# Low-rank projection of the decay gates: three token blocks at once on three groups of 32 columns

## What is computed

```
h   = RMSNorm_pre(x) * (1 + scale) + shift
z   = h @ W_in         # columns: q | k | v | g | lr_f | lr_b | u
la_f = log_sigmoid(lr_f @ w_a2[0] + b_a2[0]) / 16      # per token, 256 channels
la_b = log_sigmoid(lr_b @ w_a2[1] + b_a2[1]) / 16
o_f, s_f = gla(q, k, v, la_f, s0_fwd)                  # chunked scan
o_b, s_b = gla(flip(q), flip(k), flip(v), flip(la_b), s0_bwd)
y = concat(rmsnorm(o_f + flip(o_b)) * silu(g), fourier(u)) @ W_out
```

## Time and profile before

| | us |
|---|---|
| three runs | 1488.44, 1487.04, 1477.68 |
| median | 1487.04 |
| span of the profiled execution, first to last instruction | 1476.2 |
| PE busy in it | 1252.9 |
| DVE busy in it | 747.0 |
| ACT busy in it | 425.2 |
| POOL busy in it | 256.6 |

### The profile page before, as it was taken

One profiled execution on the slowest core, in us unless ns is written; L12 is line 12 of the kernel. 1 busy time (PEld: TensorE's weight loads), 2 busy tenths in 40 slices (PEclk: granted clock), 3 DMA queues, 4 the chain that ended last, 5 costly groups with the idle time before them and its releaser, 6 DMA issues.

```text
span 1476.2 us, 18755 instructions
## 1 busy us (share of the span) xinstructions
PE 1252.9 (85%) x7319; PEld 736.4 (50%) x7319; DVE 747.0 (51%) x1093; ACT 425.2 (29%) x736; POOL 256.6 (17%) x416
## 2 busy tenths in 40 slices
PE   3449999999862338976879999999999999999995
PEld 2225568886651314433445454454554545546442
DVE  3364583892652434755545444444545354454537
ACT  4354352322111215643333032130311312213103
POOL 1111120430212111112211111202112111121104
PEclk9779999999785768988989999999999999999998
DMA  9822011434300220000011110101011010111003
GB/s 294 266 92 63 29 58 37 147 112 147 118 29 0 105 109 29 1 14 16 29 57 34 54 57 30 58 30 57 32 55 58 29 57 29 58 39 48 29 0 128
DMA packets 70751, 97.24 MB, mean 66 GB/s; under 512 B 3077, under 2 KB 53386, under 8 KB 70666
## 3 DMA queue, kind: packets, MB, share of 16 engines
q1 hardware_dynamic: 70666, 96.04, 19.9%
HBM read 86.33 MB, written 9.70 MB: 65 GB/s over the span
## 4 chain that ended last, share of the span: by engine, by line
PE 47%; issue 2%; DVE 1%; POOL 1%; ACT 1%; POOLq 0%; ACTq 0%; DVEq 0%
PE bank L1202 47%; ACT bank L866 1%; POOL region L833 1%; DVE region L2055 0%; POOL small L757 0%; DVE region L2026 0%; POOL small L677 0%; DVE region L1953 0%; DVE ghb L1953 0%; ACT whi L554 0%; DVE region L2057 0%; DVE region L1942 0%; POOL small L755 0%; ACT region L1115 0%; ACT region L1120 0%
## 5 line engine op out<-in xcount | busy, mean ns | idle before, releaser
L1202 PE MATMUL bank<-region,whi 128*128 128x384 f16 (+1 forms) x1872 | 460.4, 328 | 47.8 <-issue 31.9
L1202 PE MATMUL bank<-whi,region 128*128 128x512 f16 (+1 forms) x1872 | 487.9, 348 | 8.9 <-DVE region L1909 8.9
L1202 PE MATMUL bank<-wlo,region 128*128 128x512 f16 (+1 forms) x936 | 325.3, 348 | 0.0
L1202 PE MATMUL bank<-region,wlo 128*128 128x384 f16 (+1 forms) x936 | 307.2, 328 | 0.0
L1202 PEld LDWEIGHTS bank<-region,whi 128*128 128x128 f16 (+1 forms) x1872 | 183.3, 98 | 174.5 <-issue 37.8
L1202 PEld LDWEIGHTS bank<-whi,region 128*128 128x128 f16 x1872 | 184.2, 98 | 170.5 <-DVE region L1909 9.8
L1202 PE MATMUL bank<-region 128*128 128x512 f16 (+8 forms) x802 | 176.0, 386 | 64.0 <-DVE region L1858 34.3
L2026 DVE SCALAR_TENSOR_TENSOR region<-bank,small,region 128x512 f32<-128x512 f32 x144 | 106.7, 749 | 180.5 <-PE bank L1202 180.1
L554 ACT ACTIVATE whi<-stage,small 128x2048 f16<-128x2048 f32 (+1 forms) x42 | 82.3, 1960 | 338.3 <-PE bank L1202 291.1
L1202 PEld LDWEIGHTS bank<-region 128*128 128x128 f16 (+4 forms) x802 | 112.7, 171 | 119.5 <-issue 48.2
L702 POOL PARTITION_ALL_REDUCE small<-small x45 | 76.3, 1695 | 407.1 <-DVE small L537 335.1
(11 more groups left out here) (152 smaller groups left out, 900.7 us busy)
## 6 DMA issues: line engine op xcount, KB each, us to landing
stage<-in_w_fc SPq DMA_DIRECT2D x32, 1024.0 KB, 5.2
stage<-in_w_ada SPq DMA_DIRECT2D x16, 1024.0 KB, 5.3
region<-in_w_ada SPq DMA_DIRECT2D x8, 1024.0 KB, 12.0
stage<-in_w_in SPq DMA_DIRECT2D x8, 1024.0 KB, 5.4
x_with_position<-region SPq DMA_DIRECT2D x9, 512.0 KB, 4.9
region<-x_with_position SPq DMA_DIRECT2D x9, 512.0 KB, 9.1
out_dram<-region SPq DMA_DIRECT2D x9, 512.0 KB, 2.6
region<-in_x_sample SPq DMA_DIRECT2D x8, 512.0 KB, 10.6
```

Of the source, the lines that this page charges most:

```text
L1202: return nc.tensor.matmul(out, lhsT, rhs, start=start, stop=stop, skip_group_check=True)
```

## The change

The three tiles of the rank stage become one bank of 96 rows: block t goes to rows 32t to 32t+31, by products placed on the columns 32t to 32t+31 of the array. The loop order is depth, term, block, so the three blocks' products of one slice and one term stand next to each other. The stage waits once for `s_tl` at 5 and halfway at 6. ACT evicts the bank in one instruction to `lrS`, now 96 rows by 384 columns. `wa2` is kept three times, at rows 0, 32 and 64, so that the logits of block t read the partitions from 32t on. Its blocks come by six small loads instead of two, POOL clears 96 rows instead of 32, and the semaphore that counts the loads is waited for at 112 instead of 48. Ring A loses two places in its list.

```diff
@@ -153,7 +153,7 @@
 
     def z_uses(i):
         if i == LR:
-            return [("z", i, 0, t) for t in range(TB)]
+            return [("z", i, 0, 0)]
         if i in TFORM:
             return [("z", i, m, t) for t in range(TB) for m in range(2)]
         return [("z", i, 0, j) for j in range(NT)]
@@ -358,8 +358,9 @@
         acc = R1[:].rearrange("p (j n) -> p j n", j=NT)
 
 
-        wa2 = R34[0:2 * RANK, 4608:4608 + 512]
-        lrS = R34[0:2 * RANK, 5120:5120 + TOK]
+        LRP = 2 * RANK * TB
+        wa2 = R34[0:LRP, 4608:4608 + 512]
+        lrS = R34[0:LRP, 5120:5120 + TBW]
 
 
         s_2h = sem("h2_high")
@@ -604,8 +605,10 @@
             sp.dma_start(ghb[:], a["g_head"][0].rearrange("h v -> (h v)").partition_broadcast(P)).then_inc(s_misc, 16)
 
             sp.wait_ge(s_wa2, 1)
-            for d in range(2):
-                sp.dma_start(wa2[RANK * d:RANK * d + RANK, 256 * d:256 * d + 256], a["w_a2"][0, d]).then_inc(s_misc, 16)
+            for t in range(TB):
+                for d in range(2):
+                    r = 2 * RANK * t + RANK * d
+                    sp.dma_start(wa2[r:r + RANK, 256 * d:256 * d + 256], a["w_a2"][0, d]).then_inc(s_misc, 16)
 
             for j in range(NT):
                 x_ready(sp, j)
@@ -777,7 +780,7 @@
             h_scale(0)
             for i in range(1, len(zin)):
                 chunk_scale(i)
-            pool.wait_ge(s_misc, 48)
+            pool.wait_ge(s_misc, 16 * (1 + 2 * TB))
             for r in range(2 * NT + 1):
                 if r < 2 * NT:
                     pool.wait_ge(s_ge, r + 1)
@@ -958,9 +961,8 @@
                 if i == LR:
                     for key in z_uses(i):
                         bank = take_z(key)
-                        t = key[3]
-                        nc.scalar.activation(lrS[:, TBW * t:TBW * t + TBW], bank[0:2 * RANK, 0:TBW], ACT.Copy,
-                                             scale=wcof[0:2 * RANK, i % 8:i % 8 + 1]).then_inc(A.read(key), 1)
+                        nc.scalar.activation(lrS, bank[0:LRP, 0:TBW], ACT.Copy,
+                                             scale=wcof[0:LRP, i % 8:i % 8 + 1]).then_inc(A.read(key), 1)
                 elif i == Q:
                     evac_t(i, qT)
                 elif i == K:
@@ -1288,15 +1290,30 @@
                              (lambda k: wh[:, k, :], lambda k: wl[:, k, :]))
 
             def logits(k):
-                pe.wait_ge(s_misc, 48)
-                for t in range(TB):
-                    A.wait_read(pe, ("z", LR, 0, t))
+                pe.wait_ge(s_misc, 16 * (1 + 2 * TB))
+                A.wait_read(pe, z_uses(LR)[0])
                 for d in range(2):
                     for t in range(TB):
                         key = ("la", d, k, t)
                         bank = B.open(pe, key)
-                        mm(bank[:, 0:TBW], wa2[:, 256 * d + P * k:256 * d + P * k + P], lrS[:, TBW * t:TBW * t + TBW],
+                        r = 2 * RANK * t
+                        mm(bank[:, 0:TBW], wa2[r:r + 2 * RANK, 256 * d + P * k:256 * d + P * k + P], lrS[r:r + 2 * RANK, :],
                            True, True).then_inc(B.filled(key), 1)
+
+            def rank_tile(key):
+
+                wh, wl = pair(LR)
+                bank = A.open(pe, key)
+                for k in range(KT):
+                    if k == KT // 2:
+                        pe.wait_ge(s_tl, 2 * TB)
+                    for n, (w, H) in enumerate(((wh, HTh), (wh, HTl), (wl, HTh))):
+                        for t in range(TB):
+                            r = 2 * RANK * t
+                            ins = nc.tensor.matmul(bank[r:r + 2 * RANK, 0:TBW], w[:, k, :], H[:, k, TBW * t:TBW * t + TBW],
+                                                   start=k == 0 and n == 0, stop=k == KT - 1 and n == 2,
+                                                   tile_position=(0, r), skip_group_check=True)
+                return ins
 
             for i in range(G_A):
                 pe.wait_ge(s_wlo, i + 1)
@@ -1304,9 +1321,8 @@
                     if i in TFORM:
                         _, _, m, t = key
                         if i == LR:
-
-                            pe.wait_ge(s_tl, 2 * t + 1)
-                            ins = up_tile(key, 0, i, m, t, HTh, HTl, 2 * RANK, lambda: pe.wait_ge(s_tl, 2 * t + 2))
+                            pe.wait_ge(s_tl, 2 * TB - 1)
+                            ins = rank_tile(key)
                         else:
                             ins = up_tile(key, 0, i, m, t, HTh, HTl)
                     else:
@@ -1771,7 +1787,7 @@
                 elif i == V_B:
                     fold()
             step(V.memset(Srf, 0.0))
-            dve.wait_ge(s_misc, 48)
+            dve.wait_ge(s_misc, 16 * (1 + 2 * TB))
             for what, n in gate_events:
                 if what == "z":
                     if n == 0:
```

## The result

| | before | after |
|---|---|---|
| median of 12 runs each, us | 1483.88 | 1474.08 |
| lowest and highest, us | 1477.02, 1488.44 | 1468.13, 1481.41 |
| ratio of after to before, with its 95% interval | | 0.9929 [0.9911, 0.9947] |
| profiled execution: span, its own time, us | 1476.2 | 1470.9, 1472.70 |

The change takes 0.71% off, 10.5 us by the ratio (the two medians are 9.8 apart); the interval runs from 0.53 to 0.89%. The forecast was 1484.7 us, 2.3 us less than the median of the three runs known then.

A forecast was written before the change was run, and what follows sets the result against it. TensorE (PE) was taken as the bound from Q's first product at 106.65 us, VectorE (DVE) releasing Q before. Q's clock (-1.3) and logits (-1.0) gave 1487.0 - 2.3 = 1484.7 us, range 1475.4 to 1492.2 us.

The forecast's parts named there:

- The rank stage: Before Q: a packed group of three costs one product, ending near 103.9 us; the 48 products saved gain nothing themselves.
- The second rival: Rank stage into Q's start: column groups run one after another, +3.8 us, 1490.8 us; chance 0.13.
- the third: Rank stage: weight loads stand between the products, Q 2.0 us late, 1488.0 us; chance 0.05.
- The step on the clock: Packed rank stage: low clock for 3.1 us of work (10 groups), then full; pause before Q 2.7 us at most.
- Q's first products: Start of Q: after the shorter pause its first 9 products run at the full clock, 1.3 us gained.
- The logits: Both sets of logits: three products run side by side until banks bind, 0.5 us gained a set, 1.0 us in all.
- it holds PE for 0.68 us: Logits: the sixth product, starting when a bank frees at 134.33 us, ends at 135.0 us instead of 135.53.
- The sum: Whole kernel: -1.3 - 1.0 = -2.3 us, put against the runs' median of 1487.0 us, giving 1484.7 us.
- The rest, at nothing: Single eviction, POOL's clearing of 96 rows, four more loads and ring places: 0 us, at worst 1.0 us from POOL.
- A microsecond taken from its queue there is a microsecond of the program: From Q's first product, for 260 us: PE is the bound, so its savings count fully if what follows only moves along.
- The forecast's case: Whole kernel: 2.3 us faster, 1484.7 us; chance 0.6.
- The first rival: Q and logits: nothing gained is on the path, Q starts at the low clock, logits wait for banks, 1487.0 us; chance 0.22.

## Why the prediction was wrong, and where it was right

**The rank stage: right, but for the clock.** Threes side by side, loads inside the products, no time gained by the 48 products saved themselves. The second rival (column groups one after another) and the third (loads between the products) are refuted by the pitch of 0.32 us. The rule of the Trainium skill behind the third ("TensorE: Matmul & The Clock Gate", "Part 3: Packing small matmuls") is contradicted by the loads of three column groups, 0.18 us together, that start while products of the same rows run. The step on the clock was wrong in its size for this trace: the low clock lasted to about 107 us, 5.75 us of work, not 3.1, so the stage ends at 108.2, and the pause is 1.56 us instead of 2.7. In the two further traces of after it is 2.75 and 2.03 us, near the forecast's, and Q's first products are at the full clock there too:

```profile
107.77 0.50 PE L1204 MATMUL bank<-region,whi 128*128 128x384 f16 x2 [2.75 <-DVE wlo L563]
```

In all traces Q is at the low clock, from its start or soon behind it, after pauses of 3.9 to 4.6 us, and at the full clock throughout after pauses of up to 2.75 us.

**Q's first products: right in the trace, mis-sized as a term.** "All of it", 1.3 us, is what the two first traces show (24.82 to 23.50). But in four traces of before Q takes 24.82 to 26.38 us, 25.56 in the mean: the term is 2.1 us. In the other three Q loses 1.7 to 2.9 us, as the low clock lasts longer than the 2.80 us read off the first.

**The logits: right in the trace, wrong as a term.** 3.51 us and 3.58 us hold PE instead of twice 4.06, 1.0 us together, and the banks bind as worked out; counted from Q's first product, K starts 1.87 us earlier, where 1.8 was forecast. The step that failed is "it holds PE for 0.68 us": that is the price at the full clock. In three of four traces of before the clock falls in these products, and then they and the first microseconds of the next projection cost more. From the logits to the end of the projections the four traces of before take 197.48 us in the mean, the three of after 192.85: the term measured 4.6 us, not 1.0.

**The sum: the step that cost the forecast.** "A difference this small is put against the median" joined a gain read in one execution to a median that this execution doesn't stand for. Its span of 1476.2 us was 1.5 us under the fastest run then known, and the prediction said so, but took it for what lies around the span. Where a run's own time and span are both known, they lie 1.8 us apart (1472.70 and 1470.9). The execution's time was thus about 1478 us, nearly the fastest of twelve and 6 us under their median. The 10.8 us from its span to the median of the first three were taken as what lies around the span, and as scatter. It should have been read as: something costs this kernel some 6 to 9 us in its usual execution that this trace doesn't show. Not all of that is the cost that the change takes away. The span is 6.2 us under the mean of the other three traces of before: 3.0 of this lie ahead of h's first low half, where nothing is edited (it starts at 83.9 us instead of 86.9), and of the 6.5 us between Q and the end of the projections some 3 are lost again in the stretch behind.

**"The rest, at nothing": right on the edits.** POOL and then SP in order of time, after, answering to the earlier trace rows:

```profile
67.10 0.52 POOL L779 MEMSET region<- 96x512 f32 x1
...
67.65 2.65 SPq L611 DMA_DIRECT2D region<-in_w_a  x6
```

96 rows are cleared in the time of 32 (0.515 us before), and six loads take 2.65 us instead of 2.4 as worked out, with Q's pace still set by DVE. The one eviction takes 0.58 us instead of 1.48 and nobody waits for it.

**"A microsecond taken from its queue there is a microsecond of the program": not borne out.** The prediction made it hang on what follows only moving along, and this does not: the stretch between the projections and the feed-forward part is no constant, as the table shows.

**What the sum didn't contain: partly open.** From the start of h's first low half to the end of the span, four traces of before take 1394.7 us in the mean, three of after 1384.4, 10.3 less; this agrees with the measured ratio. Of it 6.7 us are the two terms above (223.0 to 216.3), 0.3 lie in the feed-forward part, and 3.4 in the stretch between (394.9 to 391.5). That is less than its spread within one kernel, and packing does not explain it by itself: the changed kernel with split logits has 399.0 and 395.1 us there, the rank stage packed alone 386.1 and 392.3. A part that varies there is a wait for the load of modulation weights. What PE waited for there, in the first trace of before, and then in the first with the rank stage packed alone (in the second it is 3.6 us again):

```profile
PE bank L1235 <- DMA stage<-in_w_ada: 3.6, 1, 3.6
```

```profile
PE bank L1239 <- DMA stage<-in_w_ada: 0.2, 1, 0.2
```

Over the 18 traces this wait is 0.2 to 4.8 us, for unpacked rank stages 1.6 to 4.8 and for packed ones 0.2 to 3.8. Whether the change has a hand in it can't be told from so few; no experiment was made on it. So a third of the gain has no cause shown. The 2.7 us by which all starts later in the first trace of after are within the scatter: h's first low half, ahead of any edited product, starts between 83.8 and 89.5 us in the four traces of before, and at 84.1 to 86.6 in the three of after.

**The chances.** The forecast's case, faster by less than 1%, is what happened, and within 1% had the most of the chance. The range was too narrow on the fast side, as it was drawn from the fastest run known then and a gain of 2.3 us. The first rival (nothing on the path) fell: Q is warm and starts its work at the full clock in all three traces of after.

## What to carry to other kernels

Before a gain is priced from one trace, set that trace's span, with what lies around it, against the median of the runs: if it is a fast execution, the usual one has a cost that the trace does not show, and a change may take that away or leave it. In this kernel part of it lay where the granted clock fell: behind a pause (3.9 to 4.6 us here), and in the float32 products of 32 rows, with TensorE busy throughout. Take two or three traces of a kernel, and follow what a stage gains or loses to the end of the program, as a later stretch may give it back. And where instructions are added for an experiment, compare the stages that they cannot touch; what changes there is not the effect under test.

## What was not expected of the hardware

- The granted clock falls to 0.50 while TensorE is busy without a gap: in the second trace of before at about 139 us, 2.5 us into twelve float32 passes of 32 rows, after 20 us of 16-bit products at the full clock. It comes back only during the following 16-bit products. The logits then take 5.22 us instead of 4.06, and K's 144 products 25.42 instead of 23.25: 3.3 us a set.
- The same program at the same place keeps the clock in one execution and loses it in another: 218.16 and 225.83 us for the same 1667 products.
- 36 instructions put in front moved the feed-forward part, some 600 us later, from 753.9 to 751.2 us: the gap of up to 1.5 us at each of two turns of a loop went away.
- Three row groups of float32 products start together: the first three logits of the changed kernel with the split hold PE for 0.85 us (131.26 to 132.11), in before with the split 2.13 (138.46 to 140.59), a factor of 2.5.
